# The second MLP by Strassen block products, with its way down taken in eighths between them

## The reference

```python
def sqrelu_mlp(h, w1, w2):
    return jnp.square(jax.nn.relu(h @ w1)) @ w2
...
        h_lat = h_lat + mod_l[5] * sqrelu_mlp(modulate(rmsnorm(h_lat, norm2_g[i]), mod_l[3], mod_l[4]),
                                              mlp_w1[i], mlp_w2[i])
...
    return rmsnorm(h_lat, final_g)
```

## Time and profile before

| | us |
|---|---|
| three runs | 1768.87, 1766.85, 1769.25 |
| median | 1768.87 |
| span of the profiled execution | 1768.5 |
| TensorE busy in it | 1747.3 (99%) |
| VectorE, ScalarE, GpSimd busy | 1091.9, 805.5, 238.7 |

### The profile page before, as it was taken

The page is one execution under the profiler, slowest core; times in us unless marked ns, Lnnn a source line. Parts: engine busy times, 40 slices in busy tenths (PEclk is TensorE's granted clock), DMA queues, the critical chain, the costliest instruction groups (busy, mean ns, idle before and its releaser), DMA issues.

```text
span 1768.5 us, 25104 instructions
## 1 busy us (share of the span) xinstructions
PE 1747.3 (99%) x8622; PEld 1449.8 (82%) x8622; DVE 1091.9 (62%) x1491; ACT 805.5 (46%) x1165; POOL 238.7 (13%) x312
## 2 busy tenths in 40 slices
PE   7999999999999999999999999999999999999998
PEld 5888888888888888888888888888988888888887
DVE  6688777775356666679855666686656653223343
ACT  4566666665322222365313534664443475225521
POOL 0111111110011210122111126121110200000011
PEclk9999999999999999999999999999999999999999
DMA  9343333332546663336565573111122323333332
GB/s 335 90 131 120 120 120 115 112 112 80 179 133 190 195 195 112 103 103 211 194 190 169 190 226 100 48 49 48 49 72 62 94 95 95 107 95 95 94 97 70
DMA packets 72128, 220.85 MB, mean 125 GB/s; under 512 B 9328, under 2 KB 19952, under 8 KB 72048
## 3 DMA queue, kind: packets, MB, share of 16 engines
q1 hardware_dynamic: 52704, 160.20, 28.5%
q0 software_dynamic: 17632, 56.83, 10.4%
q10 hardware_dynamic: 1712, 2.75, 0.5%
HBM read 217.52 MB, written 2.23 MB: 124 GB/s over the span
## 4 chain that ended last, share of the span: by engine, by line
PE 94%; DVE 3%; ACT 1%; DMA 1%; DVEq 1%; SPq 1%; issue 0%; ACTq 0%
PE bank L416 23%; PE bank L418 23%; PE bank L417 23%; PE bank L1319 3%; PE bank L1321 3%; PE bank L1320 3%; PE bank L1370 1%; PE bank L1372 1%; PE bank L1371 1%; PE bank L1603 1%; PE bank L447 1%; PE bank L449 1%; PE bank L448 1%; PE bank L1599 1%; PE bank L654 1%; PE bank L1576 0%
## 5 line engine op out<-in xcount | busy, mean ns | idle before, releaser
L382 ACT ACTIVATE whi<-wraw 128x1024 fp32r<-128x1024 f32 x278 | 294.3, 1060 | 448.9 <-PE bank L418 334.0
L402 DVE TENSOR_TENSOR wlo<-wraw,whi 128x1024 fp32r<-128x1024 f32 x278 | 345.9, 1246 | 192.5 <-ACT whi L382 174.2
L416 PE MATMUL bank<-uhi,whi 128*128 128x512 f32 x1140 | 446.1, 391 | 0.0
L418 PE MATMUL bank<-uhi,wlo 128*128 128x512 f32 x1140 | 443.7, 389 | 0.0
L417 PE MATMUL bank<-ulo,whi 128*128 128x512 f32 x1140 | 443.6, 389 | 0.0
L416 PE MATMUL bank<-vhi,whi 128*128 128x512 f32 x648 | 253.0, 390 | 0.0
L417 PE MATMUL bank<-vlo,whi 128*128 128x512 f32 x648 | 252.1, 389 | 0.0
L418 PE MATMUL bank<-vhi,wlo 128*128 128x512 f32 x648 | 252.1, 389 | 0.0
L418 PEld LDWEIGHTS bank<-uhi,wlo 128*128 128x128 f32 x1140 | 214.0, 188 | 44.9
L417 PEld LDWEIGHTS bank<-ulo,whi 128*128 128x128 f32 x1140 | 214.1, 188 | 43.7
L416 PEld LDWEIGHTS bank<-uhi,whi 128*128 128x128 f32 x1140 | 214.1, 188 | 43.7
...
## 6 DMA issues: line engine op xcount, KB each, us to landing
wraw<-in_units SPq DMA_DIRECT2D x280, 512.0 KB, 3.6
...
x<-in_xT SPq DMA_DIRECT2D x4, 512.0 KB, 5.9
...
```

Source lines behind the costliest of these rows:

```text
L382: act.activation(whi[:, at % SLOTS, :], wraw[:, at % RAW, :], ACT.Copy).then_inc(w_hi, 1)
L402: dve.tensor_tensor(wlo[:, at % SLOTS, :], wraw[:, at % RAW, :], whi[:, at % SLOTS, :].bitcast(f32), ALU.subtract).then_inc(w_split, 1)
L416: pe.matmul(out, wh, rhs_hi(k), start=first and k == 0, stop=False)
L418: mm = pe.matmul(out, wl, rhs_hi(k), start=False, stop=last and k == KT - 1)
```

## The change

The second MLP alone is rewritten. The first four inner tiles are made as before (`up2a` is now one step of four units). The other 28 are made in 14 quads of two tiles. A quad's weights are a 1024 x 256 block, seen as 2 x 2 blocks of 512 x 128; its input u is seen as 2 x 2 blocks of 512 features by 256 tokens. In place of eight block products there are seven, by Strassen's scheme in Winograd's form. A product is 4 k-tiles x 3 matmuls of 256 columns. Here P0 to P6 are the seven products of a quad; they accumulate in three banks XB, YB and ZB, and what a bank holds between products is copied or added out.

What comes with that:

- GpSimd forms four sums of weight blocks per quad (`quad_sums`, S1 to S4, each 128 x 512) in the quad's source buffer (`qsrc`, 2 buffers).
- ScalarE rounds seven left operands per quad (`quad_hi`, ring of 8) and VectorE takes their rests (`quad_lo`, written over the source).
- Four sums of u, the turned operands `tf`, are formed once: two on VectorE, two on GpSimd, each 128 x 1024; ScalarE rounds them (`thi`), VectorE takes the rests (`tlo`).
- Two u tiles' worth of partial results per quad are moved by four ScalarE copies and three VectorE adds of 256 columns, and then squared, rounded and rested.
- The way down is taken in eighths of the inner layer: 4 inner tiles, 8 outputs, four outputs per quad. D0 to D3 are a quad's four down blocks, 12 matmuls of 512 columns each, standing between its products. Each is added into `xr` at once (`down_dve`). The last four outputs of the last eighth are done in two token halves.
- The norm now keeps its float32 result (`u32`), since the sums need it.
- The loads of quad 1 go where `u32` lies, and so wait until all four turned sums are formed.
- The loops of this stage are written out.

The heart of the diff:

```diff
-    ("up2a", 4, [0, 1, 2, 3], 4), ("down2a", 4, [0, 1], 4),
-    ("up2b", 4, [0, 1, 2, 3], 4), ("down2b", 4, [0, 1], 4),
+    ("up2a", 4, [0, 1, 2, 3], 1), ("down2", 4, [0, 1, 2, 3] * 2, 8),
...
+        def pair_load(sp, n):
+            at, (unit, col) = M0 + 4 + n, down_pair(n)
+            sp.wait_ge(w_split, at - RAW + 1)
...
+        def mlp2_loads(sp):
+            pair_load(sp, 0)
+            sp.wait_ge(unit_done, M0)
+            quad_top(sp, 0)
+            quad_low(sp, 0)
+            for n in (1, 2, 3):
+                pair_load(sp, n)
+            q_wait(sp, "t_dve", 2)
+            q_wait(sp, "t_pool", 2)
+            quad_top(sp, 1)
+            quad_low(sp, 1)
+            pair_load(sp, 4)
+            for g in range(QUADS):
+                pair_load(sp, 2 * g + 5)
+                if g + 2 < QUADS:
+                    q_wait(sp, "done", PRODUCTS * g + 3)
+                    quad_top(sp, g + 2)
+                if 2 * g + 6 < 32:
+                    pair_load(sp, 2 * g + 6)
+                if g + 2 < QUADS:
+                    q_wait(sp, "done", PRODUCTS * g + 7)
+                    quad_low(sp, g + 2)
+
+        def quad_sums(pool, g):
+            w = qsrc[g % 2]
+            q_wait(pool, f"top{g % 2}", 16 * (g // 2 + 1))
+            q_wait(pool, f"low{g % 2}", 16 * (g // 2 + 1))
+            pool.tensor_tensor(w[:, S1, :], w[:, 2, :], w[:, A22, :], ALU.add).then_inc(Q["sum"], 1)
+            pool.drain()
+            pool.tensor_tensor(w[:, S2, :], w[:, S1, :], w[:, A11, :], ALU.subtract).then_inc(Q["sum"], 1)
+            pool.tensor_tensor(w[:, S3, :], w[:, A11, :], w[:, 2, :], ALU.subtract).then_inc(Q["sum"], 1)
+            pool.drain()
+            pool.tensor_tensor(w[:, S4, :], w[:, A12, :], w[:, S2, :], ALU.subtract).then_inc(Q["sum"], 1)
...
+        def mlp2_pool(pool):
+            quad_sums(pool, 0)
+            norm_m.ready(pool, KT)
+            pool.tensor_tensor(tf[:, 2], u32[:, 4:8, HALVES[1]], u32[:, 0:4, HALVES[1]], ALU.subtract
+                               ).then_inc(Q["t_pool"], 1)
+            q_wait(pool, "t_dve", 2)
+            pool.tensor_tensor(tf[:, 3], u32[:, 4:8, HALVES[0]], tf[:, 1], ALU.subtract).then_inc(Q["t_pool"], 1)
+            pool.drain()
+            for g in range(1, QUADS):
+                quad_sums(pool, g)
...
+        def quad_pe(pe, at, out, rhs_hi, rhs_lo, first):
+            g, n = at // PRODUCTS, at % PRODUCTS
+            q_wait(pe, "lo", at + 1)
+            for t in range(4):
+                wh = qhi[:, at % 8, t * P:(t + 1) * P]
+                wl = qlo[g % 2][:, LEFT[n], t * P:(t + 1) * P]
+                pe.matmul(out, wh, rhs_hi(t), start=first and t == 0, stop=False, skip_group_check=True)
+                pe.matmul(out, wh, rhs_lo(t), start=False, stop=False, skip_group_check=True)
+                mm = pe.matmul(out, wl, rhs_hi(t), start=False, stop=t == 3, skip_group_check=True)
+            mm.then_inc(Q["done"], 1)
...
+        def mlp2_pe(pe):
+            for g in range(QUADS):
+                at = PRODUCTS * g
+                q_wait(pe, "act", 4 * g)
+                straight_pe(pe, at, XB, 0, 0, True)
+                q_wait(pe, "dve", 3 * g - 1)
+                turned_pe(pe, at + 1, ZB, 0, True)
+                straight_pe(pe, at + 2, YB, 4, 0, True)
+                down_pe(pe, g, 0)
+                q_wait(pe, "act", 4 * g + 1)
+                turned_pe(pe, at + 3, XB, 1, False)
+                q_wait(pe, "act", 4 * g + 2)
+                straight_pe(pe, at + 4, ZB, 4, 1, False)
+                down_pe(pe, g, 1)
+                q_wait(pe, "act", 4 * g + 3)
+                turned_pe(pe, at + 5, XB, 2, False)
+                down_pe(pe, g, 2)
+                q_wait(pe, "dve", 3 * g + 3)
+                turned_pe(pe, at + 6, XB, 3, False)
+                down_pe(pe, g, 3)
```

More of the change, by code:

```diff
@@ L468, in __init__ @@
                 self.shift_at = shift_at
+                self.kept = full is not None
+                self.full = full or (lambda j: nsq[:, j % 2, :self.n])
             def ready(self, eng, tiles):
@@ L1129, in step @@
                     half = k % 2
-                    if last is not None and isinstance(it, int) and it == 3 and k == 2:
-                        last()
-                        return
                     pe.wait_ge(N2["r_l"], done + 8 + 8 * half)
```

557 lines of the change are left out of this document (439 added, 118 removed).

## The result

| | before | changed |
|---|---|---|
| median of the runs, us | 1769.06 (1766.85 to 1769.96, 4 runs) | 1777.69 (1776.32 to 1780.60, 4 runs) |
| profiled execution, span | 1768.5 | 1775.4 |
| ratio to before | | 1.0051, 95% 1.0039 to 1.0064 |

The kernel became slower by 0.5%. Each run that lists both has its time 1.6 to 2.4 us above its own span, so the 0.4 us between the median and the span before is not what lies around a span: by this the profiled execution of before took 1770.1 to 1770.9 us, more than each of its four runs (an estimate). The page of the changed kernel, against the earlier trace rows: fewer busy microseconds on TensorE (1740.4 for 1747.3), yet its part in the chain that ended last has fallen from 94% to 84%; VectorE, DMA and waits have taken the rest.

The account below looks back on a forecast made before the run. The prediction took TensorE, busy 1747.3 of 1768.5 us, to bound the kernel. Its sum was 1768.5 - 11.2 (products) + 16.75 (start) + 0.45 (eighths and tail) = 1774.5 us of span, 1774.9 us as median; range 1765 to 1783.

Parts of the forecast that it names:

- Saving, 11.2 us: TensorE products: seven narrow-matmul products replace eight blocks, saving 0.80 us a quad over 14 quads, -11.2 us.
- the 109.2 of the prediction: TensorE matmuls of 256 columns: 109.2 ns by the skill's formula, set aside for the 120.0 ns in the rows.
- Taking turns: VectorE instructions with two SBUF inputs and GpSimd's run one behind the other; +3.8 us in the norm.
- The start, 16.75 us: Norm to P6 of quad 0: P6 at 1465.3 against 1448.55 without any wait, costing 16.75 us.
- One chain: Start of the stage: VectorE, load, GpSimd, ScalarE, VectorE form one chain, so its waits are not added to each other.
- The later quads without a wait: Quads after the start: period 20.96 us, no TensorE wait, smallest slack 1.5 us before P6.
- rival C: Later quads wait too, from loads 3 us late or slower GpSimd sums: 1783 us; chance 0.13.
- The tail: Kernel's end after the last matmul: one more mean matmul and VectorE busy with the other half, +0.15 us.
- The sum: Whole kernel: 1768.5 - 11.2 + 16.75 + 0.45 = 1774.5 us of span, 1774.9 us as median.
- A: Port free, VectorE doesn't wait for GpSimd: the start costs 8.35 us, time 1766.5, no change; chance 0.14.
- B: TensorE's four units and ten blocks hide the start: wait 2.7 us, time 1760.8 us, faster; chance 0.08.
- D: Idle before P5 drops TensorE's clock to 1.2 GHz, lasting into quad 1: 3.7 us lost, 1778.6; chance 0.15.

Follow-up runs that it names:

- e4: Changed kernel with each quad's DMA queue sending quad g+2's low load ahead of the pair's load; ratio to before 1.0037.
- e3: Changed kernel with GpSimd's four sums of quad 0 after the last norm, not beside it; one run, path 371.8 us against 372.6.
- e1: Changed kernel with quad 0's XB copy, rounding and rest of A and add of XB ahead of quad 1's work; ratio to before 1.0056.
- e5: Changed kernel with e1's and e4's edits, quad 1's loads ahead of pairs 2 to 4, quad 2's ahead of pairs 5 and 6; ratio to before 1.0016.
- e12: e5 without quad 1's early loads, plus earlier XB adds, quad 0's last XB copy earlier, quad 1's adds ahead of five rests; ratio to before 1.0011.

## Why the prediction came out right, and where it did not

- **Saving, 11.2 us.** The narrow matmuls start 120 ns apart, as taken from the rows. The Trainium skill (TensorE: Matmul & The Clock Gate, section Back-to-back issue gap) gives the formula behind the 109.2 of the prediction for an isolated matmul, which the prediction did not say, and about 131 ns at 512 columns for a stream with weight loads. Neither agrees with the 120 and 226.7 ns here. But e4's periods without a wait are 21.04 us against 20.96: a down block next to products takes 2.75, not 2.72. Over 13 periods 1.0 us less, about 1.1 over all 14, so about 10.1 were saved.
- **Taking turns.** Right, and shown by e3. The norm's last rest came 3.3 us late (forecast 4.1, the 0.35 of the split among them), 1024 columns on GpSimd took 2.41 (2.4).
- **The start, 16.75 us.** Measured 15.7 (58.27 against a wait-free 42.58). P5's wait was 6.78 with its releaser as forecast (6.8). P6 came 8.2 us behind P5 (8.3) for the reason forecast, VectorE's work ahead of the add of XB. The waits before P0 and P1 were 0.78 and 0.73, one of 2.3 in the forecast, and the one before D0 0.40 (0.8).
- **One chain.** The forecast had VectorE, load, GpSimd and ScalarE in one chain and did not add the waits. e1 shows that this was true beyond quad 0: of 8.6 us won there 7.7 were lost by P6 of quad 1 and the rest by P6 of quad 2.
- **The later quads without a wait.** This step failed. The forecast had "loads land at 3.9" and a slack of 1.5 us. The first sum starts 4.7 to 6.3 us behind P6, the slack is 0 to 0.36, and P6 came 3.7 us late in all. e4 names the cause, the pair's load ahead of the low load in the queue, and gives the 3.7 back. It is rival C's mechanism at less than half of its price. The forecast had counted the low load as if nothing were in flight ahead of it. With nothing ahead (e4) the first sum does start at 3.9 to 4.4, and the add of XB starts 14.0 us behind it (14.05 in the forecast). P6 can start 0.5 us behind that start and no sooner, which the 1.5 left out, so even e4's slack is 0.66 to 1.21 us.
- **The tail.** Last P6 to the end: 37.06 us; the forecast's sum leaves 36.7 for it.
- **The sum.** On the path the forecast was +6.0 and the result +10.1: -1.1 at the start, +4.8 in the later quads (3.7 of waits, 1.0 of period), +0.3 at the end. That the forecast of the profiled span, 1774.5, stands only 0.9 from 1775.4 owes 3.2 us to the execution: its first 100 us had more clock than the one before was profiled with. Against the medians (+8.6) it was 2.8 us too low. The 0.4 us from span to median did no harm: it is too small as a distance (1.6 to 1.7 us in the changed kernel's runs), but it takes the span of before to its median. That the time came out this close is luck in part: the start, 1.1 us too dear, hid some of the 4.8 us that the later quads cost.
- **The rivals.** A (no turns) falls by e3. B (covered start, a wait of 2.7 us) is out by the 15.7 measured, and e5 to e12 show that no order tried gets it: the nearest path is 0.9 us over before. D's low clock came where it was forecast and ended earlier than forecast, in the middle of D2 (0.50 up to 1458.1, then full), so D did not come true. The forecast of nothing for the clock holds, but only because VectorE's add came 1.37 us later still.

What stays open: how much of the last 7.4 us of start waits (e12: 1.2, 0.8, 0.7, 0.4 and 4.25) would go without the turns with GpSimd, and how much with a still better order. The rows say that 3.1 us of turns stand ahead of the last wait; no run takes these sums away, and the rest that D0 waited for, whose tile was rounded by 1479.2, was not moved ahead of the three rests in front of it. So it is not shown that VectorE's own work is a floor.
